# Query and key projections of the forgetting attention by the Strassen scheme, a key and a query tile as the halves of rows

## The reference, cut to what matters

```python
def mixer_inputs(xn, pos, w_in, b_fgate):
    z = xn @ w_in
    ...
    fq, fk, fv, fz, dq, dk, dv, gate_fox, gate_dil = jnp.split(z, cuts, axis=-1)
    logf = jax.nn.log_sigmoid(fz.astype(jnp.float32) + b_fgate.astype(jnp.float32))
...
    fox_kv_p.append(jnp.stack([fk, fv], axis=2))
```

## Time and profile before

| | us |
|---|---|
| median of 3 runs | 2626.5 |
| the three runs | 2625.26 to 2635.47 |
| the profiled execution, its own time | 2628.53 |
| span of the profiled execution, first to last instruction | 2626.7 |
| TensorE busy | 2591.1 (99%) |
| TensorE's weight loads | 1821.2 (69%) |
| VectorE busy | 1195.6 (46%) |
| ScalarE busy | 521.2 (20%) |
| GpSimd busy | 178.4 (7%) |
| chain of work that ended last | TensorE 95%, DMA 2% |

### The profile page before, as it was taken

The page is one execution under the profiler, slowest core; times in us unless marked ns, Lnnn a source line. Parts: engine busy times, 40 slices in busy tenths (PEclk is TensorE's granted clock), DMA queues, the critical chain, the costliest instruction groups (busy, mean ns, idle before and its releaser), DMA issues.

```text
span 2626.7 us, 37785 instructions
## 1 busy us (share of the span) xinstructions
PE 2591.1 (99%) x14338; PEld 1821.2 (69%) x14338; DVE 1195.6 (46%) x2902; ACT 521.2 (20%) x1143; POOL 178.4 (7%) x284
## 2 busy tenths in 40 slices
PE   8999999999999999999999999999999999999999
PEld 7655656666656666676445886558888888888887
DVE  2155653332253333343553443355666666654432
ACT  2233323221202222121011112311211212110002
POOL 1000001232202222000000000000000000000000
PEclk9999999999999999999999999999999999999999
DMA  5000101100117888787215104433544452162101
GB/s 199 23 13 10 62 1 58 62 20 21 49 29 232 267 260 259 233 267 238 111 48 202 42 1 165 153 82 116 185 142 136 148 163 68 33 202 94 66 31 69
DMA packets 208474, 299.22 MB, mean 114 GB/s; under 512 B 20941, under 2 KB 145246, under 8 KB 207254
## 3 DMA queue, kind: packets, MB, share of 16 engines
q1 hardware_dynamic: 149462, 192.47, 22.5%
q10 hardware_dynamic: 42976, 89.26, 10.6%
q0 software_dynamic: 15856, 15.07, 2.3%
HBM read 270.43 MB, written 65.71 MB: 128 GB/s over the span
## 4 chain that ended last, share of the span: by engine, by line
PE 95%; DMA 2%; DVE 1%; ACT 1%; ACTq 1%; issue 1%; SPq 0%; DVEq 0%
PE psum L2853 22%; PE psum L3235 11%; PE psum L1068 10%; PE psum L2048 8%; PE psum L536 5%; PE psum L2136 4%; PE psum L2535 4%; PE psum L1424 3%; PE psum L2237 3%; PE psum L2056 3%; PE psum L707 3%; PE psum L724 2%; PE psum L2513 2%; PE psum L1440 2%; PE psum L1460 2%; PE psum L735 1%
## 5 line engine op out<-in xcount | busy, mean ns | idle before, releaser
L2853 PE MATMUL psum<-arena 128*128 128x272 f32 x2464 | 568.0, 394 | 1.2 <-DVE arena L2927 1.2
L2853 PEld LDWEIGHTS psum<-arena 128*128 128x128 f32 x2464 | 469.9, 191 | 98.6 <-issue 1.3
L3235 PE MATMUL psum<-arena 128*128 128x256 f32 (+1 forms) x1584 | 288.1, 356 | 0.0
L1068 PE MATMUL psum<-arena 128*128 128x512 f32 (+3 forms) x960 | 284.6, 458 | 0.0
L2048 PE MATMUL psum<-arena 128*128 128x368 f32 (+1 forms) x768 | 279.1, 475 | 0.9 <-DVE arena L1984 0.6
L3235 PEld LDWEIGHTS psum<-arena 128*128 128x128 f32 (+1 forms) x1584 | 252.4, 178 | 34.7 <-issue 3.2
L1068 PEld LDWEIGHTS psum<-arena 128*128 128x128 f32 (+1 forms) x960 | 150.2, 179 | 89.1 <-issue 78.3
L2048 PEld LDWEIGHTS psum<-arena 128*128 128x128 f32 x768 | 127.8, 190 | 52.0 <-issue 14.8
L2956 DVE TENSOR_TENSOR arena<-arena,psum 128x272 f32<-128x272 f32 (+2 forms) x330 | 111.8, 378 | 112.7 <-PE psum L2853 112.0
L1424 PEld LDWEIGHTS psum<-arena 128*128 128x128 f32 x848 | 105.0, 141 | 69.1 <-issue 46.3
L2977 DVE SCALAR_TENSOR_TENSOR arena<-arena 128x1024 f32<-128x1024 f32 x88 | 113.1, 1285 | 52.6 <-ACT arena L2879 51.1
(11 more groups left out here) (274 smaller groups left out, 2950.6 us busy)
## 6 DMA issues: line engine op xcount, KB each, us to landing
arena<-in_cache_fox_kv ACTq DMA_DIRECT2D x128, 256.0 KB, 4.7
arena<-in_cache_fox_kv SPq DMA_DIRECT2D x128, 256.0 KB, 5.0
out_win_s<-in_cache_win_kv ACTq DMA_DIRECT2D x8, 4080.0 KB, 15.0
arena<-in_w_up SPq DMA_DIRECT2D x44, 512.0 KB, 6.5
arena<-in_w_down SPq DMA_DIRECT2D x14, 1408.0 KB, 6.2
arena<-in_cache_win_kv SPq DMA_DIRECT2D x16, 1024.0 KB, 8.6
arena<-in_cache_mem_kv SPq DMA_DIRECT2D x16, 1024.0 KB, 6.3
out_y_p<-arena SPq DMA_DIRECT2D x20, 512.0 KB, 2.7
```

What stands on the lines that cost most here:

```text
L1068: last = pe.matmul(banks[c0 // 512][p0:p0 + r, 0:n], xn_tile(k, g, t), wD[g][:, k, w0:w0 + n], start=(k == 0), stop=(k == KD - 1))
L2853: last = pe.matmul(bank_of(j, x, p), w[:, k, :], r[:, k, Q4 * p:Q4 * p + Q4], start=(k == 0), stop=(k == 3))
L3235: last = pe.matmul(down_out(u)[p0:p0 + r, 0:n], hT(f)[:, tok + t * P:tok + t * P + r], slot[slots[c]][:, f - fa, c0:c0 + n], start=(f == f ...
```

## The change

For each pair the key and the query columns are stacked as the two halves of rows of one product, the 1088 tokens as two halves of 544 columns and the 1024 channels as two halves of the inner dimension. The 2 x 2 x 2 block product is made by the Strassen scheme in Winograd's form: seven products in place of eight. Each product is made in two parts p of 272 columns, four matmuls each.

- Sums of tokens T1 to T4 are made once (pair_token_sums_dve), of weight blocks s1, s2, s4 and an overwritten block for each pair (pair_weight_sums, pair_fourth_sum), all on VectorE. A scale of 1/8 for the queries is worked into them.
- VectorE adds each product after the first onto KT, QT or an intermediate u2 while it drains the bank; ScalarE drains the first product and the bias units. The samples' queries go through q_new to qbF.
- Units use banks 0, 1 and 2 in turn. A pair's keys are turned in the stage of the next pair; those of pair 3 in a stage of their own behind p3 (foxpair 4), and the first matmul of d0 waits for their copies (k_kept 12).
- T1 lies where lf_raw lies. The 128 page loads are therefore due from 302 and wait for the last product of pair 3; their transposes are due at 445 and 452, the suffix sums behind them.
- The weights of d0 are due a little later and wait for the product that last reads the region.

```diff
+        QT2, QT4 = TOK // 2, TOK // 4
+        SUMS, COPIES = 16, 7
+        PRODUCTS = [("product", x, p) for x in range(7) for p in range(2)]
+        SPREADS = [("bias", n, 0) for n in range(4)]
+        K_TURNS = [("turn", n, 0) for n in range(3)]
+        PAIR_UNITS = [PRODUCTS + SPREADS]
+        PAIR_UNITS += [PRODUCTS[0:4] + K_TURNS[0:1] + PRODUCTS[4:6] + K_TURNS[1:2] + SPREADS + K_TURNS[2:3] + PRODUCTS[6:]
+                       for j in range(3)]
+        PAIR_UNITS += [K_TURNS]
...
+        k_t1, k_t2, k_t3 = [take(4 * QT2, a).rearrange("p (k t) -> p k t", k=4) for a in (B2 + 4 * TOK, f0 + 34432, f0 + 15872)]
...
+            w = (a11, s2, a12, a21, a22, s1, s4)[x]
+            return w[:, k, :], t4 if x == 4 else (k_b11, k_t2, k_b21, k_t3, None, k_t1, k_b22)[x][:, k, cols]
...
+                if kind == "turn":
+                    yield pair_at(j, i)
+                    pe.wait_ge(*nth(qk, "summed", SUMS * j))
+                    pair_drained(pe, q - 3)
+                    for n in range(4 if x < 2 else 1):
...
+                        if q == 2:
+                            pe.wait_ge(s_vec, 2)
+                            pe.wait_ge(*nth(qk, "t_sums", 4))
+                        if x == 1 and p == 0:
+                            pe.wait_ge(*nth(qk, "w_sums", 4 * j + 3))
+                        if x == 3 and j == 0:
+                            pe.wait_ge(*nth(qk, "t_sums", 6))
+                        if x == 4 and j == 0:
+                            pe.wait_ge(*nth(qk, "t_sums", 9))
+                        if x == 6 and p == 0:
+                            pe.wait_ge(*nth(qk, "w_sums", 4 * j + 4))
+                        if q >= 3:
+                            pair_drained(pe, q - 3)
+                    w, r = pair_operands(j, x, k, p)
+                    last = pe.matmul(banks[q % 3][:, 0:QT4], w, r, start=(k == 0), stop=(k == 3))
+                last.then_inc(qk["s"]["computed"], 1)
...
+        def pair_token_sums_dve(dve):
+            for p in range(2):
+                yield at("norm1")(1) + 2 * p
+                dve.wait_ge(*nth(n1, "kept", 2 * (7 if p == 0 else TT)))
+                c = slice(QT4 * p, QT4 * p + QT4)
+                dve.tensor_tensor(k_t1[:, :, c], k_b12[:, :, c], k_b11[:, :, c], ALU.subtract).then_inc(qk["s"]["t_sums"], 1)
+                dve.wait_ge(*nth(qk, "t_sums", 2 * p + 1))
+                dve.tensor_tensor(k_t2[:, :, c], k_b22[:, :, c], k_t1[:, :, c], ALU.subtract).then_inc(qk["s"]["t_sums"], 1)
+            yield at("p0")(0) - 2
+            pair_weight_sums(dve, 0)
+            yield at("p0")(0) + 1
+            dve.wait_ge(fp["v_computed"], TT)
+            for p in range(2):
+                c = slice(QT4 * p, QT4 * p + QT4)
+                dve.tensor_tensor(k_t3[:, :, c], k_b22[:, :, c], k_b12[:, :, c], ALU.subtract).then_inc(qk["s"]["t_sums"], 1)
+            dve.wait_ge(*nth(qk, "t_sums", 4))
+            dve.tensor_tensor(k_t4, k_b21[:, 0:3, :], k_t2[:, 0:3, :], ALU.subtract).then_inc(qk["s"]["t_sums"], 1)
...
+            pair_fourth_sum(dve, 0)
...
+                for dst, c0, c1 in parts:
+                    was = dst if base is None else base(c0, c1)
+                    got = bank[:, c0:c1]
+                    if scaled:
+                        last = dve.scalar_tensor_tensor(out=dst, in0=got, scalar=-QSCALE, in1=was, op0=ALU.mult, op1=ALU.add)
+                    else:
+                        last = dve.tensor_tensor(dst, was, got, ALU.add)
+                last.then_inc(qk["s"]["summed"], 1)
...
+                if j < 3 and (x, p) == (4, 0):
+                    pair_weight_sums(dve, j + 1)
+                if j < 3 and (x, p) == (5, 0):
+                    pair_fourth_sum(dve, j + 1)
...
         def dilproj_sp(sp, g):
-            yield at(f"d{g}")(0) - 40 if g else at("p3")(0.6)
+            yield at(f"d{g}")(0) - 40 if g else at("p3")(0.9)
...
                             if t == 0 and g == 0:
-                                pe.wait_ge(fp["copied"], 4 * PAIR - (0 if c0 else 1))
+                                pe.wait_ge(*nth(qk, "summed", 4 * SUMS))
+                                pe.wait_ge(fp["k_kept"], 12)
...
             for n in range(NB * NPG):
-                yield at("p0")(0) + 0.3 * n
+                yield at("p3")(1) + 4 + 0.3 * n
                 if n == 0:
                     sp.wait_ge(s_ptab, 16)
+                    sp.wait_ge(*nth(qk, "computed", PAIR_FROM[4]))
...
+        def lf_turn_at(n):
+            return at("d1")(0) + 5 + 7 * n
...
+                if n == 0:
+                    pe.wait_ge(s_lf, 16 * NB * NPG)
+                    pe.wait_ge(*nth(dp[0], "kept", TT))
...
         def suffix_dve(dve):
-            yield at("p3")(0.5)
+            yield lf_turn_at(2) + 2
```

## The result

The changed kernel takes 2642.8 us (median of four runs, 2640.7 to 2644.9) against 2625.9 us. The ratio is 1.0057, 95% interval 1.0031 to 1.0082: **slower by 15 us**, where 25 us were forecast. The difference is small, but its interval leaves out no difference. The time lies in the forecast range, it moved the way that was forecast and for the reason named, but the size is off by 10 us. The profiled execution has a span of 2639.6 us against 2626.7, so the two traces differ by 12.9 us.

A forecast was written before the change was run, and what follows sets the result against it. TensorE, busy 2591.1 of 2626.7 us, was taken as the bound. Products' end -10.0, second window's start +31.1, transposes +0.9 and low clock +3 gave +25.0: 2626.5 + 25.0 = 2651.5 us, range 2638 to 2665.

The forecast's parts named there:

- end T of pair 3's products: Last projection product of pair 3 on TensorE: moves from 314.3 us by -14.4 - 1.0 - 0.9 + 1.3 + 5 = -10.0 us.
- start of the second window, relative to T: Second window projection waits for weights queued behind 128 page loads: starts 31.1 us later, counted from pair 3's last product.
- transposes and low clock: Around the second window: eight log-forget transposes 0.9 us, and slow matmuls after the long wait 3 us.
- all later stages: Stages behind the second window's added costs: the forecast sum holds no term for them.
- The columns: Projection products of four pairs: 56 matmuls a pair at 0.458 us, 102.6 us in place of 117.0, saving 14.4 us.
- the moved turns: Key transposes come one pair later, those of pair 3 after its last product: 1.0 us leaves the stretch before that.
- VectorE: the term that was mis-sized: Added sums during the pairs stall TensorE: 1.3 us in pair 0, 5 us in pairs 1 to 3; VectorE about 75% busy.
- The queue: SyncE after pair 3's last product: rope table, 128 page loads, then second window weights, landed 172.9 us behind that product.
- The rival by which the loads are hidden: SyncE's page loads under 1.06 us each, or weights passing them: no wait for weights, -3.6 us, 2623 us; chance 0.13.
- The hole at the first window: TensorE idles about 4.5 us before the first window projection, for pair 3's last sum, copies and a store; swallowed later.
- The clock: After 25 us without a matmul, TensorE may run at half rate: 3 us taken, bounds 0 and 4; skill's rule 2.
- busy and idle memory: SyncE's 128 page loads before the change: 1.257 us each through both memory states, a price kept for the moved loads.

The follow-up runs named there:

- the small dose: Changed kernel with one more VectorE maximum over 512 columns ahead of every added sum; one execution, 2649.8 us; first to last product 219.1 us.

## Why the prediction was right, and where not

The forecast's terms against the two traces (us):

| step | forecast | measured | from |
|---|---|---|---|
| end T of pair 3's products | -10.0 | -18.5 | rope table at 314.36, then 295.89 |
| start of the second window, relative to T | +31.1 | +30.8 | 456.05 - 314.36, then 468.42 - 295.89 |
| transposes and low clock | +3.9 | +3.1 | see below |
| all later stages | 0 | -2.6 | see below |
| sum | +25.0 | +12.9 | spans |

**The columns: right.** A product's matmul of 272 columns was forecast at 0.458 us; in pair 0, 33 of them run without a break from 95.02 to 110.25, 0.46 us each. Of the 18.0 us by which the products' stretch is shorter, 14.4 are the columns by the forecast's price (13.6 at 15.23 / 33 = 0.4615), 1.0 the moved turns by the forecast and 0.8 the moved log-forget transposes (the kernel before with the loads moved has 232.0 for 232.8).

**VectorE: the term that was mis-sized.** I forecast 1.3 us of stall in pair 0 and 5 in the others. There is none: pair 0 is 33.0 us from product to product of pair 1, as the sum without a stall gives, and the stretch is even 1.8 us shorter than the moved work explains. I charged half of the added work at worst and a sixth as likely from the first microsecond on, while the changed kernel shows no stall at 69% of VectorE. The load was forecast too high as well. Pairs 1 to 3 after, in the columns of the earlier trace rows:

```profile
113.70:295.80 182.10, 181.39 (x1162) 124.14 (x1160) 128.65 (x381) 65.31 (x147) 6.40 (x9) 1.00 0.09 27
```

That is 71% and not 75%, and 19 us more of VectorE than before (109.5) and not 31: pair 3 makes no weight sums for a next pair, and the copies and the suffix sums of the log-forgets, 4.0 us, have left it. With the small dose these pairs stand at 79% and do lose. What I hadn't priced was gain on ScalarE. The four bias units of pair 0 took 3.60 us from start to start (114.98 to 118.58) and now 3.44 (110.25 to 113.69), 0.6 us over 16 if the others do alike; the 1.4 us of waits of the turned probabilities for ScalarE are gone. Together that is 2.0, about what is left over (1.8, or 2.6 with the columns at 13.6); that ScalarE's fewer copies are the cause of the second part I argue, no run parts it.

**The queue: right to 0.4 us, in part by luck.** The chain rope table, 128 x 1.25, issue, landing came to 172.9 and is 172.5: the weights are issued at T + 161.4 and not T + 162.4, and land 11.1 us later and not 10.5, and the two misses nearly cancel. The rival by which the loads are hidden wanted 1.06 us a load. It is 1.26 again, and the trace splits it: reading the page number 0.49, register operations 0.24, the DMA instruction 0.25, the rest issue. The hole at the first window was forecast at 4.5 us and is 3.9 in two pieces (0.53 and 3.33), swallowed as said. TensorE is ready for the second window at T + 148.7 and not T + 147.3, so the wait is 23.8 us and not 25.6, with no effect on the time.

**Behind it.** From the start of the second window to that of the gates it is 225.9 us before and 229.1 after: +3.1, forecast 3.9. The clock: ten records of 512 columns take 6.46 us from 468.42 to 474.88 where they take 4.29 without a gap ahead of them (444.34 to 448.63 with 64 loads), 2.2 us lost. The granted clock of the stretch:

```profile
469.00:475.00 6.00, 6.00 (x12) 2.41 (x11) 0.00 (x0) 0.00 (x0) 0.00 (x0) 0.70 0.00 0
```

0.70 is a mix of the levels 1.2 and 2.4 GHz, after 23.8 us without a matmul; from 475 on it stands at 1.00. The Trainium skill (TensorE: Matmul & The Clock Gate, Part 1: The HAM clock gate) says that idling brings the half rate and sustained work lifts it; by that rule I had estimated 2 us, and it is closer than the 3 that I took from the start of the trace.

**Later stages.** Nothing was forecast, and the first trace gives back 2.6 us between the gates and the up projection (first starts 682.0 and 1755.2 before, 697.5 and 1768.1 after). That stretch is 1070.6 us in this profile and 1074.7 in the second one of the same kernel, against 1073.2 in the kernel before; with the key wait narrowed, which touches nothing in it, it is 1081.9 (698.1 to 1780.0). So this is the scatter of executions and no gain that can be shown. It may also be why the spans' 12.9 us stand below the 15 us of the times.

So of the 12.1 us between the forecast and the spans, 6.3 are stalls that are not there, about 2 an unpriced gain, 1.1 the queue and what stands behind it, and 2.6 scatter.

## What to carry to other kernels

When a load is moved because its region is taken, go through everything that stands behind it on its new place of the queue; a due time moves neither its length nor its end, and here 128 loads of 4 KB cost more than a Strassen step saves. The same change is a gain of 0.4% with the loads split around the one weight load that is urgent, and of 0.7% with the wait for the key copies narrowed too, so a slower time spoke against its placing and not against the scheme. Price added work on a second engine by where that engine stands: nothing at 69% here, a sixth of each microsecond from there to 79%, over half of it from 79 to 85%. These are numbers of this weave, and of work put ahead of its drains.

## What was unexpected of the hardware

- The clock also falls in a short gap: with 112 page loads TensorE stands still for 7.0 us, and the ten records behind it take 5.9 us (451.19 to 457.10) in place of 4.3; the granted clock is 0.73 from 451 to 457 and 1.00 from 457 on:

```profile
451.00:457.00 6.00, 5.81 (x10) 2.65 (x11) 0.00 (x0) 0.00 (x0) 2.92 (x6) 0.73 0.04 6
```

  After 23.8 us they take 6.5 and after 30.9 us 6.7 (487.22 to 493.96), so a gap over four times as long loses 0.8 us more.
- A load whose page number SyncE reads first costs SyncE 1.25 us, though its DMA instruction is 0.25: 128 in 159.8 us with the DMA engines 4% busy, 160.9 us in the kernel before with them 7% busy. By the rows of the queue it is SyncE's own time; no run has such loads beside a busy memory, so the prediction's words "busy and idle memory" say more than its rows.
- Three loads of 1 MB landed 11.1 us after the first issue in the changed kernel and 12.5 us with 112 page loads, for 10.5 forecast; why they differ is open.
